# Where the matmul operands of a two-block transformer kernel lie within the 256-byte rows of the on-chip memory

## The reference

```python
# first block (T = 272 positions)
proj = rmsnorm(h) @ w_in                    # neighbourhood attention and latent attention
h = h + concat(rmsnorm(out_a), rmsnorm(out_b)) @ w_out
h = h + (silu(conv3(hn @ w_gate)) * (hn @ w_up)) @ w_down            # D_FF 5632
# second block (256 positions), modulated by c @ w_ada
proj = h2 @ w_in_2                          # 9 parts: conv branch, hgrn branch, two gates
y_a = (a_b * causal_conv(a_c * a_x)) @ w_conv_out
y_b = (rmsnorm(hgrn(q, f, i)) * silu(g_out)) @ w_hgrn_out
x = x + gt_m * ((sigmoid(gate_a) * y_a + sigmoid(gate_b) * y_b) @ w_o)
x = x + gt_f * ((silu(h2 @ w_ffn_gate) * (h2 @ w_ffn_up)) @ w_ffn_down)   # D_FF 5632
return rmsnorm(x)
```

## Time and profile before

| | |
|---|---|
| three runs | 2705.64 us median, 2702.92 to 2707.32 |
| the profiled execution | 2700.86 us, its span 2699.5 us |
| TensorE matmul busy | 2645.3 us, 98% of the span, 22052 instructions |
| weight loads busy | 2606.7 us |
| VectorE, ScalarE, GpSimd busy | 1844.0, 1248.4, 331.5 us |
| DMA | 571.22 MB, mean 212 GB/s |
| mean granted TensorE clock | 0.995 |

### The profile page before, as it was taken

How to read it: one execution, slowest core, us unless ns; L and a number is a source line. 1 busy time by engine, 2 the same in 40 slices (tenths; PEclk the granted TensorE clock), 3 DMA queues, 4 the chain that set the end, 5 groups by cost and what they waited for, 6 DMA issues and landing times.

```text
span 2699.5 us, 51384 instructions
## 1 busy us (share of the span) xinstructions
PE 2645.3 (98%) x22052; PEld 2606.7 (97%) x22052; DVE 1844.0 (68%) x2592; ACT 1248.4 (46%) x1943; POOL 331.5 (12%) x526
## 2 busy tenths in 40 slices
PE   7999999999999999999999999999999999999998
PEld 7888889999999999999999999999999999999998
DVE  6666568877777777787888667776877644444444
ACT  5556655544433444445444443334554443444443
POOL 2110101111121111231000001110211000000001
PEclk9999999999999999999999999999999999999999
DMA  6433345678788887886444568886768656555553
GB/s 204 137 106 103 118 148 173 205 267 269 263 293 278 277 270 262 272 285 207 152 147 155 188 225 279 273 279 217 256 208 273 219 192 191 195 188 190 187 186 126
DMA packets 500084, 571.22 MB, mean 212 GB/s; under 512 B 26704, under 2 KB 473424, under 8 KB 499856
## 3 DMA queue, kind: packets, MB, share of 16 engines
q1 hardware_dynamic: 467968, 463.76, 52.6%
q0 software_dynamic: 31600, 103.80, 11.9%
q10 hardware_dynamic: 288, 0.36, 0.1%
HBM read 565.77 MB, written 2.54 MB: 211 GB/s over the span
## 4 chain that ended last, share of the span: by engine, by line
PE 86%; DVE 7%; ACT 4%; issue 1%; DMA 1%; POOL 0%; SPq 0%; DVEq 0%; ACTq 0%
PE ps L704 27%; PE ps L705 27%; PE ps L706 26%; DVE wl L1811 3%; ACT wh L1301 2%; PE ps L1002 1%; PE ps L833 1%; DMA raw<-in_w_in 1%; DVE nx L1915 1%; DVE lr L2007 1%; ACT lp L1476 0%; PE ps L806 0%; PE ps L858 0%; PE ps L859 0%; PE ps L671 0%
## 5 line engine op out<-in xcount | busy, mean ns | idle before, releaser
L1811 DVE TENSOR_TENSOR wl<-raw,wh 128x1024 fp32r<-128x1024 f32 (+1 forms) x894 | 1058.9, 1200 | 577.0 <-ACT wh L1301 572.7
L1301 ACT ACTIVATE wh<-raw 128x1024 fp32r<-128x1024 f32 (+1 forms) x894 | 883.2, 1030 | 606.1 <-PE ps L706 587.8
L704 PE MATMUL ps<-xs,wh 128*128 128x256 f32 x2880 | 811.3, 282 | 5.8 <-DVE xs L1892 5.8
L705 PE MATMUL ps<-xs,wh 128*128 128x256 f32 x2880 | 799.4, 278 | 0.0
L706 PE MATMUL ps<-xs,wl 128*128 128x256 f32 x2880 | 796.7, 277 | 0.0
L704 PEld LDWEIGHTS ps<-xs,wh 128*128 128x128 f32 x2880 | 539.9, 187 | 7.6 <-DVE wl L1811 5.8
L705 PEld LDWEIGHTS ps<-xs,wh 128*128 128x128 f32 x2880 | 545.0, 189 | 1.0 <-issue 1.0
L706 PEld LDWEIGHTS ps<-xs,wl 128*128 128x128 f32 x2880 | 539.5, 187 | 0.0
L704 PE MATMUL ps<-xx,wh 128*128 128x258 f32 (+3 forms) x1840 | 530.2, 288 | 3.7 <-DVE xx L1894 3.7
L705 PE MATMUL ps<-xx,wh 128*128 128x258 f32 (+3 forms) x1840 | 522.3, 284 | 0.0
L706 PE MATMUL ps<-xx,wl 128*128 128x258 f32 (+3 forms) x1840 | 522.3, 284 | 0.0
(11 more groups left out here) (378 smaller groups left out, 2753.2 us busy)
## 6 DMA issues: line engine op xcount, KB each, us to landing
raw<-in_w_in SPq DMA_DIRECT2D x118, 1024.0 KB, 5.3
ada_raw<-in_w_ada POOLq DMA_DIRECT2D x384, 256.0 KB, 4.8
raw<-in_w_gate SPq DMA_DIRECT2D x44, 1024.0 KB, 6.5
raw<-in_w_up SPq DMA_DIRECT2D x44, 1024.0 KB, 7.1
raw<-in_w_ffn_gate SPq DMA_DIRECT2D x44, 1024.0 KB, 5.2
raw<-in_w_ffn_up SPq DMA_DIRECT2D x44, 1024.0 KB, 5.3
raw<-in_w_down SPq DMA_DIRECT2D x32, 1024.0 KB, 6.0
raw<-in_w_ffn_down SPq DMA_DIRECT2D x32, 1024.0 KB, 5.4
```

Source lines behind the costliest of these rows:

```text
L704: pe.matmul(dst, h[:, c, o:o + w], x[:, 0, k, g.t0:g.t1], start=(k == 0), stop=False)
L705: pe.matmul(dst, h[:, c, o:o + w], x[:, 1, k, g.t0:g.t1], start=False, stop=False)
L1301: act.activation(wh[i % NS][:, part], raw[i % NR][:, part], ACT.Copy).then_inc(s_hi, 1)
L1811: dve.tensor_tensor(wl[i % NS][:, part], raw[i % NR][:, part], wh[i % NS][:, part].bitcast(F32), ALU.subtract).then_inc(s_lo, 1)
```

## The change

`rstd` and two `ssq` tiles, which stood between `wh` and `wl`, move behind `sqt`, so that `wl` has the residue of `wh`, 128. `xx` follows `wl` directly, now also at 128. `xs`, `hid` and `conv` get a home at `wh_off - 128`, residue 0, and their chunks from 1 on lie 16 elements (64 bytes, `LEAD`) further than before: chunk 0 at residue 0, all others at 64. The planes of `hid` and `conv` are 64 elements (256 bytes) longer to hold that, `xs` keeps its size. `oo` begins at `wh_off - 64`, residue 64, with no shift after its first chunk. The helper `led(x, h, c)` gives the slice of chunk c. No instruction is added or taken away, none changes its engine, its shape or its waits.

```diff
+LEAD = 16
+HID_PLANE = HALF * 256 + 64
+CONV_PLANE = 8 * 256 + 64
...
         wh = [sb(f"wh{i}", [P, SLAB], F32R) for i in range(NS)]
-        rstd = sb("rstd", [P, T])
-        ssq = {n: sb(f"ssq_{n}", [P, T]) for n in "ha"}
-        assert (cursor[0] - wh_off) % ROW_BYTES == 192
+        assert (cursor[0] - wh_off) % ROW_BYTES == 0
         wl = [sb(f"wl{i}", [P, SLAB], F32R) for i in range(NS)]
...
-        xs, _ = at("xs", [P, 2, KD + 1, SEQ], F32R, row_home(xoff, wh_off + 64))
+        xs, _ = at("xs", [P, 2, (KD + 1) * SEQ], F32R, row_home(xoff, wh_off - 4 * (LEAD + 16)))
...
-        ffn_home = row_home(arena, wh_off + 64)
+        ffn_home = row_home(arena, wh_off - 4 * (LEAD + 16))
-        hid = sb("hid", [P, 2, HALF, SEQ], F32R)
+        hid = sb("hid", [P, 2, HID_PLANE], F32R)
-        cursor[0] = mix_home = row_home(arena, wh_off + 64)
-        conv = sb("conv", [P, 2, 8, SEQ], F32R)
-        cursor[0] = oo_home = row_home(cursor[0], wh_off + 64)
+        cursor[0] = mix_home = row_home(arena, wh_off - 4 * (LEAD + 16))
+        conv = sb("conv", [P, 2, CONV_PLANE], F32R)
+        cursor[0] = oo_home = row_home(cursor[0], wh_off - 64)
...
+        def led(x, h, c):
+            o = c * SEQ + (LEAD if c else 0)
+            return x[:, h, o:o + SEQ]
+
+        def moving(g, h, k):
+            return led(LED[g.operand], h, k) if g.operand in LED else OPERAND[g.operand][:, h, k, g.t0:g.t1]
...
-                            pe.matmul(dst, h[:, c, o:o + w], x[:, 0, k, g.t0:g.t1], start=(k == 0), stop=False)
-                            pe.matmul(dst, h[:, c, o:o + w], x[:, 1, k, g.t0:g.t1], start=False, stop=False)
-                            m = pe.matmul(dst, l[:, c, o:o + w], x[:, 0, k, g.t0:g.t1], start=False, stop=end)
+                            pe.matmul(dst, h[:, c, o:o + w], moving(g, 0, k), start=(k == 0), stop=False)
+                            pe.matmul(dst, h[:, c, o:o + w], moving(g, 1, k), start=False, stop=False)
+                            m = pe.matmul(dst, l[:, c, o:o + w], moving(g, 0, k), start=False, stop=end)
```

More of the change, by code:

```diff
@@ L349, in build @@
         sqt = [sb(f"sqt{i}", [P, T]) for i in range(2)]
-        ssq["b"] = sb("ssq_b", [P, T])
+        rstd = sb("rstd", [P, T])
+        ssq = {n: sb(f"ssq_{n}", [P, T]) for n in "hab"}
         ada_off = cursor[0]
@@ L392, in build @@
         raw_in, _ = at("raw_in", [P, 2, KD, T], F32R, limit // 32 * 32 - 8 * KD * T)
-        ffn_home = row_home(arena, wh_off + 64)
-        raw_ffn = [at(f"raw_ffn{i}", [P, 2, 8, T], F32R, ffn_home + (2 + 22 * i) * SEQ * 4)[0] for i in range(2)]
-        raw_mix, _ = at("raw_mix", [P, 2, 6, T - Q0], F32R, ffn_home + 2 * HALF * SEQ * 4)
+        ffn_home = row_home(arena, wh_off - 4 * (LEAD + 16))
+        raw_ffn = [at(f"raw_ffn{i}", [P, 2, 8, T], F32R, ffn_home + (2 * SEQ + 64 + i * HID_PLANE) * 4)[0] for i in range(2)]
+        raw_mix, _ = at("raw_mix", [P, 2, 6, T - Q0], F32R, ffn_home + 2 * HID_PLANE * 4)
         cursor[0] = ffn_home
-        hid = sb("hid", [P, 2, HALF, SEQ], F32R)
+        hid = sb("hid", [P, 2, HID_PLANE], F32R)
         gct = [sb(f"gc{i}", [P, SEQ]) for i in range(NGC)]
-        cursor[0] = mix_home = row_home(arena, wh_off + 64)
-        conv = sb("conv", [P, 2, 8, SEQ], F32R)
-        cursor[0] = oo_home = row_home(cursor[0], wh_off + 64)
+        cursor[0] = mix_home = row_home(arena, wh_off - 4 * (LEAD + 16))
+        conv = sb("conv", [P, 2, CONV_PLANE], F32R)
+        cursor[0] = oo_home = row_home(cursor[0], wh_off - 64)
         oo = sb("oo", [P, 2, 8, SEQ], F32R)
@@ L421, in build @@
         cy2 = sb("cy2", [P, 2, SEQ])
-        OPERAND = {X0: xx, XS: xs, XQ: cqx, XKV: ckvx, XB: xb, XHID: hid, XOC: conv, XOH: oo}
+        OPERAND = {X0: xx, XQ: cqx, XKV: ckvx, XB: xb, XOH: oo}
+        LED = {XS: xs, XHID: hid, XOC: conv}
+        def led(x, h, c):
[3 more added lines that the diff above has]
+            return led(LED[g.operand], h, k) if g.operand in LED else OPERAND[g.operand][:, h, k, g.t0:g.t1]
         NORM_DST = [xx, cqx, ckvx, xb, xx, xx]
@@ L457, in norm_dst @@
         def norm_dst(n, h, i):
-            return NORM_DST[n][:, h, i, NORM_T0[n]:T] if n < N_MIX2 else xs[:, h, i, :]
+            return NORM_DST[n][:, h, i, NORM_T0[n]:T] if n < N_MIX2 else led(xs, h, i)
         def norm_gain(n, i):
@@ L682, in gemm @@
                 g = GEMMS[key]
-                x = OPERAND[g.operand]
                 n = g.t1 - g.t0
@@ L1659, in ffn @@
                                 act.wait_ge(s_slab, done((b, "down", 0, 7)))
-                            act.activation(hid[:, 0, 2 * g + j, :], gct[u % NGC][:, :], ACT.Copy).then_inc(s_hidh, 1)
+                            act.activation(led(hid, 0, 2 * g + j), gct[u % NGC][:, :], ACT.Copy).then_inc(s_hidh, 1)
                     for g in range(8):
@@ L1750, in scalar_program @@
                     act.wait_ge(*last_use(("ab", p), j))
-                    act.activation(conv[:, 0, 2 * p + j, :], cy[:, j, :], ACT.Copy).then_inc(s_och, 1)
+                    act.activation(led(conv, 0, 2 * p + j), cy[:, j, :], ACT.Copy).then_inc(s_och, 1)
             lanes.drain("hgrn")
@@ L1758, in merged_split @@
                     act.wait_ge(s_mg, c + 1)
-                    act.activation(xs[:, 0, c, :], merged[:, c, :], ACT.Copy).then_inc(s_mgh, 1)
+                    act.activation(led(xs, 0, c), merged[:, c, :], ACT.Copy).then_inc(s_mgh, 1)
             for gs in [(g,) for g in range(6)] + [(6, 7)]:
@@ L2256, in ffn @@
                             dve.wait_ge(s_hidh, u + 1)
-                            dve.tensor_tensor(hid[:, 1, 2 * g + j, :], gc[:, :], hid[:, 0, 2 * g + j, :].bitcast(F32), ALU.subtract).then_inc(s_hidl, 1)
+                            dve.tensor_tensor(led(hid, 1, 2 * g + j), gc[:, :], led(hid, 0, 2 * g + j).bitcast(F32), ALU.subtract).then_inc(s_hidl, 1)
                     if b == 2 and f == 0:
@@ L2420, in vector_program @@
                     dve.wait_ge(s_och, c + 1)
-                    dve.tensor_tensor(conv[:, 1, c, :], y, conv[:, 0, c, :].bitcast(F32), ALU.subtract).then_inc(s_ocl, 1)
+                    dve.tensor_tensor(led(conv, 1, c), y, led(conv, 0, c).bitcast(F32), ALU.subtract).then_inc(s_ocl, 1)
             lanes.drain("hgrn")
@@ L2427, in merged_low @@
                 dve.wait_ge(s_mgh, c + 1)
-                dve.tensor_tensor(xs[:, 1, c, :], merged[:, c, :], xs[:, 0, c, :].bitcast(F32), ALU.subtract).then_inc(s_mgl, 1)
+                dve.tensor_tensor(led(xs, 1, c), merged[:, c, :], led(xs, 0, c).bitcast(F32), ALU.subtract).then_inc(s_mgl, 1)
             def merged_split():
```

## The result

The changed kernel takes 2717.63 us (median of five, 2716.44 to 2720.46) against 2704.86 us for the kernel before (five runs, 2702.92 to 2707.32): a ratio of 1.0053, 95% interval 1.0041 to 1.0064. The interval leaves 1 out, so the change did slow the kernel. The forecast was 2678 us, faster. The time lies in its range, 2660 to 2737, only because the range had been stretched to take in the slow rival, given 0.3.

A forecast was written before the change was run, and what follows sets the result against it. TensorE, busy 98% of the span, was taken to bound the kernel. From the profiled 2700.9 us, less 29.6 plus 2.1 gave 2673.4; with the runs' median 4.8 us above that execution, 2678 us, range 2660 to 2737.

The forecast's parts named there:

- the slow rival: Rival: at residue 64 with these weights, matmul starts lock in the even 117.7 ns cycle; 2735 us, chance 0.3.
- What bounds the kernel, and that addresses matter: Step: TensorE, busy 98% of the span, sets the time; `xx` at 118.3 ns against `xs` at 115.6 shows placement matters.
- That the starts can lock in more than one cycle, and what the two paces would be: Step: one set of addresses can lock in either pattern; bounds for the 12852 matmuls at 64 were 112.5 and 117.7 ns.
- I take 113.3 ns.: Step: the pace chosen for constant operands at residue 64 with weights at 128, nearer the short step than the mean.
- The 29.6 us of the sum: Term: gain of 2.3 ns on each of 12852 matmuls on `xs`, `hid`, `conv` and `oo` at residue 64.
- The second pace of `xs`: Reading: 96 matmuls on the same `xs` with the same weights at 117.7 ns each, in the kernel before.
- The rival of half a gain: Rival: part of the products lock in the short pattern, part don't, for instance at waits between slabs; 2693 us, chance 0.1.
- Pace as before: Rival: addresses do not carry over, the mean stays 115.6 ns and only chunk 0 costs; 2708 us, chance 0.1.
- Chunk 0: Term: the 780 matmuls of chunk 0 at residue 0 run at 118.3 ns, 2.1 us more.
- `xx` and the rest: Term: walking operands (5520 matmuls on `xx`, some 1800 others) keep their mix; taken as nothing, plus or minus 7 us.
- The other engines, DMA: Term: ACT, DVE and DMA have room for the faster pace; cost nothing, at most 5 us if DMA binds.
- The page's rule of two ports that don't disturb each other: Page rule cited for pace as before: independent ports for moving operand and weights, so placement can't matter; 118.3 against 115.6 ns opposed it.

## Why the prediction was wrong, step by step

*What bounds the kernel, and that addresses matter.* Right. TensorE's pace was all that changed, and the 12852 matmuls were the right ones to count: quick against slow in the last 4224 is worth 19 us by itself (4224 x 4.4 ns).

*That the starts can lock in more than one cycle, and what the two paces would be.* Right. The slow bound, 117.7 ns, was read from a row, and 117.8 was measured. The 113.3 ns was no reading but a choice between 112.5 and the mean; that a pace of 113.3 exists, to 0.1 ns, is luck.

*"I take 113.3 ns."* This step failed. It set out one step that should repeat because all three matmuls stand in one relation. All three do repeat one step, but two steps can repeat at these addresses, and the relation doesn't choose between them. The reason given for the choice was "just the entry that a shifted chunk 0 gives each product", from one short step in `xx`. But `xx` comes to 64 by 192 and 0 and behind a different past. Chunk 0 at 0 behind a product at 64 hands on what it finds: slow after slow, quick after quick. The runs put in its place that the start time of a product decides, and that of the entries tried only the one by 192 and then 0 ended quick after slow as well (nine of nine on `xs` and `conv` in the two runs that have it; by 192 alone 19 of 20 stayed slow). The 29.6 us of the sum were thus got on 22% of the chunks; on the others the rival's 2.1 to 2.2 ns were lost. With 0.22 x 2.3 - 0.78 x 2.2 = -1.2 ns on 12852 the sum gives 16 us more, and 2 us for chunk 0 make 18; the two spans differ by 16.0.

*The slow rival.* Right in its mechanism and its price. In the last stages it holds entirely (117.8 ns). The second pace of `xs` at unchanged addresses was the evidence that mattered, and it deserved more than 0.3. The five steps of 118 ns in the quickest chunk of `xx`, also named for it, were made with `wl` at 64 and said little of the new placement: in the changed kernel the 256-column chunk of `xx` at 64 takes 0.69 us, its last four steps 113 and 114 ns. What this rival missed is that both patterns share one execution.

*The rival of half a gain.* Its mechanism, part of the products in one pattern and part in the other, with the change at breaks, is the one that the trace shows, and it had only 0.1. Its price was wrong: it left the products that miss the short pattern at the old pace, 115.6 ns, where they fell to 117.8, and it took a half where 22% of the chunks were quick. That makes 2693 us a gain in the forecast and a loss in the measurement.

*Pace as before.* Out: the chunks of the changed kernel settle at 113.3 or 117.8 ns, not at 115.6.

*Chunk 0.* Right: six matmuls of most chunks 0 take 0.71 us, 118.7 ns each, for the 118.3 taken.

*`xx` and the rest.* Within its bounds. In the undisturbed stage of the first network (gate and up, second half) the time fell from 253.3 to 252.0 us. That came with `wl` at 128: the run with `wl` back at 64 takes 253.4 again. The changed kernel, then that run:

```profile
851.10:1103.10 252.00, 252.00 (x2134) 252.00 (x2134) 198.10 (x269) 112.35 (x152) 44.88 (x84) 1.00 0.81 270
853.10:1106.50 253.40, 253.40 (x2135) 253.40 (x2134) 198.19 (x269) 112.51 (x152) 45.11 (x84) 1.00 0.81 269
```

The first half took 1.5 us more in the changed kernel; why stays open.

*The other engines, DMA.* Right: each of TensorE's waits is within 0.3 us of before in the changed kernel, and within 2 us in all the others, the quick ones too; the last four stages show none in any of them.

*The page's rule of two ports that don't disturb each other.* By SBUF — State Buffer of the Trainium skill, section Who interferes with whom, TensorE's two read ports are independent. In the run with `hid` at 192 as before and `wl` moved, only the place that line 706's weight loads read from has changed for that stage, and each matmul takes 2.3 ns more: the measurement decides against reading that rule as one of equal speed at any address. By TensorE: Matmul & The Clock Gate of the Trainium skill (Back-to-back issue gap) 109.2 ns would be the step for 256 columns, an estimate by the page, which gives its formula for a single matmul by itself and not for a stream with a weight load before each; the quickest lasting step in any run here was 113.3.

What stays open is what in the hardware ties a load's and an operand's residues to a cycle of starts. The runs show the cycles, that the start of a product selects between them, and their prices, not their cause.

## What to carry to other kernels

When a long stream of equal matmuls bounds a kernel, divide a clean stage's length by its count before and after: if one set of addresses shows two lasting values, there is a locked pattern, and its history must be controlled as well as its addresses. Judge a placement by several products in a row and several runs, not by one short step or by one execution. A way in that turns the bad pattern into the good one at the head of each product (here two chunks at other residues) was worth more than the placement itself: the same placement of the bulk gave 2718, 2711, 2687 and 2680 us with four different heads, the kernels before them 2702 to 2705. Look at each head where a product follows a slow one without a break: of the two heads that won, one (2680) turned such products and the other (2687) mostly just kept what came out of a break.

## What the runs showed of the hardware

One extra matmul of 0.1 us changed the pace of the 4224 that followed by 4.4 ns each, for 480 us, with no wait anywhere. At 64 for activations and 128 for all weights TensorE repeats a step of 113.3 ns or of 117.8; at 192 and 128 almost always 117.8, but once 113.3 for 60 matmuls in a row; at 64 with weights at 128 and 64 only 117.8 lasted; at 192 with weights at 128 and 64 a cycle of three steps mostly averages 115.6; at 0 and 128 the steps average 118.7. In each of these stretches the granted clock was 1.00 of full, its 2.4 GHz level.
